# The seam between the mixers and the out pass: four raw buffers for the out weights, its first loads moved ahead of the barrier

## The reference

```python
mix = concat([y_a, y_b, y_c], -1) @ w_out          # 2048 -> 1024
x = x + rmsnorm(mix, norm_post_mix)
h = rmsnorm(x, norm_pre_ffn)
ff = (silu(h @ w_gate) * (h @ w_up)) @ w_down
return x + rmsnorm(ff, norm_post_ffn)
```

## Time and profile before

| | |
|---|---|
| median of 3 runs | 2977.15 us (2973.31 to 2978.05) |
| the profiled execution | 2977.66 us, its span 2975.5 us |
| TensorE busy | 2878.5 us, 97% of the span |
| VectorE, ScalarE, GpSimd busy | 64%, 40%, 13% |
| mean granted TensorE clock | 0.988 of full speed |

### The profile page before, as it was taken

How to read it: one execution, slowest core, us unless ns; L and a number is a source line. 1 busy time by engine, 2 the same in 40 slices (tenths; PEclk the granted TensorE clock), 3 DMA queues, 4 the chain that set the end, 5 groups by cost and what they waited for, 6 DMA issues and landing times.

```text
span 2975.5 us, 36083 instructions
## 1 busy us (share of the span) xinstructions
PE 2878.5 (97%) x13608; PEld 2314.3 (78%) x13608; DVE 1914.9 (64%) x2608; ACT 1195.8 (40%) x2005; POOL 385.7 (13%) x496
## 2 busy tenths in 40 slices
PE   8999999999999989999799999999999999999998
PEld 4888887777777667777688778888788888888887
DVE  4778787666853358888334576666776666656656
ACT  5322222354443445454333533333533333545443
POOL 0000000012530136655012100000000000000000
PEclk9999999999999999999899999999999999999999
DMA  4222343446765757876679744444542223766863
GB/s 154 68 68 90 125 132 111 136 140 198 225 202 164 254 185 244 285 264 246 251 250 347 262 181 160 155 163 160 202 166 107 107 106 135 276 219 198 296 192 107
DMA packets 294569, 545.14 MB, mean 183 GB/s; under 512 B 59228, under 2 KB 150780, under 8 KB 284924
## 3 DMA queue, kind: packets, MB, share of 16 engines
q1 hardware_dynamic: 262636, 437.69, 44.2%
q0 software_dynamic: 24704, 75.52, 6.6%
q10 hardware_dynamic: 7056, 29.63, 2.6%
HBM read 358.30 MB, written 184.44 MB: 182 GB/s over the span
## 4 chain that ended last, share of the span: by engine, by line
PE 46%; DMA 2%; DVE 2%; ACT 1%; issue 0%; SPq 0%; DVEq 0%; ACTq 0%
PE f_banks L2835 26%; PE f_banks L2843 14%; PE f_banks L2014 6%; DMA f_h_raw<-hq 1%; DMA hq<-o_tq 0%; PE f_banks L2210 0%; DMA f_bop1lo<-hq 0%; DMA f_raw<-in_w_gu 0%; DMA o_ident<-in_ident 0%; DMA f_bop6lo<-hq 0%; DVE f_bop1lo L2638 0%; DVE f_w_op L2645 0%; DVE f_snap L2671 0%; ACT f_w_op L2520 0%; ACT f_snap L2534 0%
## 5 line engine op out<-in xcount | busy, mean ns | idle before, releaser
L2843 PE MATMUL f_banks<-f_d_op 128*128 128x512 f32 x1848 | 419.0, 389 | 0.0
L2843 PEld LDWEIGHTS f_banks<-f_d_op 128*128 128x128 f32 x1848 | 347.0, 188 | 71.9
L2709 DVE TENSOR_TENSOR f_d_op<-f_d_raw,f_d_op 128x1024 fp32r<-128x1024 f32 x154 | 187.6, 1225 | 148.9 <-ACT f_d_op L2552 148.0
L1848 PE MATMUL t_banks<-t_w_hi,h_hi 128*128 128x512 f32 (+1 forms) x640 | 249.6, 390 | 8.1 <-DVE t_w_lo L1709 7.9
L656 PE MATMUL t_banks<-h_hi,c_w_hi 128*128 128x512 f32 x640 | 255.7, 400 | 0.0
L656 PE MATMUL t_banks<-h_hi,c_w_lo 128*128 128x512 f32 x640 | 249.9, 390 | 0.0
L656 PE MATMUL t_banks<-h_lo,c_w_hi 128*128 128x512 f32 x640 | 249.1, 389 | 0.0
L2552 ACT ACTIVATE f_d_op<-f_d_raw 128x1024 fp32r<-128x1024 f32 x154 | 162.8, 1061 | 198.3 <-PE f_banks L2843 163.5
L1848 PE MATMUL t_banks<-t_w_lo,h_hi 128*128 128x512 f32 (+1 forms) x640 | 238.6, 373 | 0.0
L1848 PE MATMUL t_banks<-t_w_hi,h_lo 128*128 128x512 f32 (+1 forms) x640 | 238.2, 372 | 0.0
L2534 ACT ACTIVATE f_snap<-f_banks 128x1024 f32<-128x1024 f32 x88 | 90.4, 1027 | 258.7 <-PE f_banks L2835 258.7
(11 more groups left out here) (399 smaller groups left out, 6299.5 us busy)
## 6 DMA issues: line engine op xcount, KB each, us to landing
f_raw<-in_w_gu SPq DMA_DIRECT2D x88, 512.0 KB, 6.3
sop<-f_a SPq DMA_DIRECT2D x154, 256.0 KB, 2.0
f_d_raw<-sop SPq DMA_DIRECT2D x154, 256.0 KB, 2.9
t_raw<-in_w_tok SPq DMA_DIRECT2D x72, 512.0 KB, 4.6
f_d_raw<-top SPq DMA_DIRECT2D x88, 256.0 KB, 4.3
m_bc<-rows SPq DMA_DIRECT2D x16, 1152.0 KB, 6.8
f_d_raw<-in_w_dn SPq DMA_DIRECT2D x66, 256.0 KB, 3.3
o_y_hi<-y_hi SPq DMA_DIRECT2D x16, 1024.0 KB, 5.2
```

The source lines that it names most:

```text
L1848: last = nc.tensor.matmul(banks[:, t, 0:width], h[:, b, k_first + k, tok], w[unit % 2][at][:, cols], start=begins and k == 0 and j == 0, s ...
L2709: tt(d_op[d % D_RING][:, 2:4], d_raw[:, d % S_RING], d_op[d % D_RING][:, 0:2].bitcast(F32), sub).then_inc(dlo_ok, 1)
L2843: last = nc.tensor.matmul(banks[:, bank, :], d_op[d % D_RING][:, s, tok], d_op[d % D_RING][:, w, :], start=k == 0 and j == 0, stop=k == FU ...
```

## The change

- Four raw buffers in place of two: groups 0 and 1 keep theirs, group 2 goes to `w_raw2`, which lies over the 2048 columns of `w_hi` that group 3's high part will take, group 3 to `w_raw3`, which lies over `work` and `gain_row`; group 4 takes buffer 0 again.
- SP asks for group 2 when the last mixer matmul that reads that memory is done (`c_mm`), ahead of y; for group 3 behind the first high part (`whi_ok` 1); for group 4 behind `whi_ok` 2 and `wlo_ok` 1.
- ACT makes group 3's high part ahead of `partial(15)` and first waits for group 2's low part (`wlo_ok` 3).
- y of tile 0: the low part is asked for right behind group 1, the high part at the old place.
- The three constants are loaded by SP in the first block, behind `wlo_ok` 4 and ahead of tile 1's y. x and `first` of tile 0 are loaded by POOL at the end of its program in the first block. TensorE's wait for the constants moves to its first transposes.
- Semaphores are shared or moved to match; the number of DMAs and of compute instructions stays.

```diff
@@ mixers
+    out_in0, out_in1 = sem("o_w_in0"), sem("o_w_in1")
+    out_w_in = (out_in0, 16), (out_in1, 32), (w_in, 16 * (NT // WM + 1)), (out_in0, 32), (out_in1, 48)
...
@@ mixers, sync, rest
             out_w(sp, 0)
             out_norm(sp)
             out_w(sp, 1)
+            sp.wait_ge(y_sent[0], 32)
+            out_y(sp, 0, (1,))
             sp.wait_ge(ve_ok, TT)
+            sp.wait_ge(c_mm, TT)
+            out_w(sp, 2)
             sp.wait_ge(y_ok, TT)
-            sp.wait_ge(y_sent[0], 32)
-            out_y(sp, 0)
-            for g in range(2, OGROUPS):
-                out_w(sp, g)
+            out_y(sp, 0, (0,))
+            out_w(sp, 3)
+            out_w(sp, 4)
+            out_const(sp)
             sp.wait_ge(acc_mm, TT)
             for b in range(2):
                 sp.wait_ge(y_sent[b], 32 * TT // 2)
@@ mixers, scalar, rest
                 elif c == TT:
                     out_upper(act, 2)
-            out_upper(act, 3)
+                    act.wait_ge(out_wlo_ok, 3)
+                    out_upper(act, 3)
             out_upper(act, 4)
@@ mixers, gpsimd, rest
+            pool.wait_ge(acc_mm, TT)
+            pool.wait_ge(part_sent[0], 16)
+            out_x(pool)
@@ out_memory
         y_hi, y_lo = [sb("y_hi0", [P, KM, P], F32R)], [sb("y_lo0", [P, KM, P], F32R)]
+        with ExitStack() as until:
+            until.enter_context(nc.sbuf_tensor("o_under_raw", [P, 24 * P * 2], F32))
+            w_raw2 = until.enter_context(nc.sbuf_tensor("o_w_raw2", [P, WG, NB], F32))
         w_hi = sb("w_hi", [P, OGROUPS * WG, NB], F32R)
...
-        first, work, gain_row, junk = sb("first", [P, 2, NB]), sb("work", [P, D]), sb("gain_row", [P, D]), sb("junk", [P, D], mybir.dt.bfloat16)
+        first = sb("first", [P, 2, NB])
+        with nc.sbuf_tensor("o_w_raw3", [P, WG, NB], F32) as w_raw3:
+            pass
+        work, gain_row, junk = sb("work", [P, D]), sb("gain_row", [P, D]), sb("junk", [P, D], mybir.dt.bfloat16)
...
+    w_raw = w_raw[:, 0], w_raw[:, 1], w_raw2[:], w_raw3[:], w_raw[:, 0]
@@ out_start
     def load_w(sp, g):
-        if g >= 2:
-            sp.wait_ge(wlo_ok, g - 1)
+        if g == 3:
+            sp.wait_ge(whi_ok, 1)
+        elif g == 4:
+            sp.wait_ge(whi_ok, 2)
+            sp.wait_ge(wlo_ok, 1)
         src = w_tiles[:, WG * g:WG * (g + 1), NB:D] if g < OGROUPS - 1 else w_tiles[:, 0:WG, 0:NB]
-        sp.dma_start(w_raw[:, g % 2], src).then_inc(w_in[g % 2], 16)
+        sp.dma_start(w_raw[g], src).then_inc(w_in[g][0], 16)
...
+    def load_const(sp):
+        sp.wait_ge(wlo_ok, 4)
+        for dst, src in ((gain_row[:], gain_mix.partition_broadcast(P)), (gain_col[:], gain_ffn), (ident_sb[:], ident)):
+            sp.dma_start(dst, src).then_inc(const_in, 16)
+
+    def load_x(pool):
+        pool.dma_start(xt[:, 0], x[0, 0:P, :]).then_inc(x_in, 16)
+        pool.dma_start(first[:, 0], first_dram[0:P, :]).then_inc(x_in, 16)
@@ out_pass
     def sync(sp, ahead):
-        for dst, src in ((gain_row[:], gain_mix.partition_broadcast(P)), (gain_col[:], gain_ffn), (ident_sb[:], ident)):
-            sp.dma_start(dst, src).then_inc(const_in, 16)
         for n in range(2, TT):
...
-        load(0)
         load(1)
...
         def transposes(n):
+            if n == 0:
+                pe.wait_ge(const_in, 48)
             pe.wait_ge(xn_ok, n + 1)
...
-        pe.wait_ge(const_in, 48)
         for n in range(1, TT):
```

More of the change, by code:

```diff
@@ L1952, in out_memory, with out_start @@
     return w_raw, y_hi, y_lo, w_hi, w_lo, late, tq, early, xt, x1, xn, first, work, gain_row, junk, ident_sb, stat, gain_col, norm_col
 def out_shared(sem):
-    return ((sem("o_w_in0"), sem("o_w_in1")), (sem("o_y_in0"), sem("o_y_in1")), sem("o_norm_in"), sem("o_whi_ok"), sem("o_wlo_ok"),
+    return ((sem("o_y_in0"), sem("o_y_in1")), sem("o_x_in0"), sem("o_const_in"), sem("o_whi_ok"), sem("o_wlo_ok"),
             sem("o_mm_ok"))
-def out_start(nc, shared, memory, w_out, norm_gain, yhi_dram, ylo_dram):
-    w_in, y_in, norm_in, whi_ok, wlo_ok, mm_ok = shared
-    w_raw, y_hi, y_lo, w_hi, w_lo, norm_col = memory[0], memory[1], memory[2], memory[3], memory[4], memory[-1]
+def out_start(nc, shared, memory, w_out, norm_gain, gain_mix, gain_ffn, ident, x, yhi_dram, ylo_dram, first_dram, w_in=None):
+    y_in, x_in, const_in, whi_ok, wlo_ok, mm_ok = shared
+    (w_raw, y_hi, y_lo, w_hi, w_lo, _, _, _, xt, _, _, first, _, gain_row, _, ident_sb, _, gain_col, norm_col) = memory
@@ L1974, in load_y, with load_norm @@
+    def load_norm(sp):
+        sp.dma_start(norm_col[:], norm_gain).then_inc(w_in[1][0], 16)
+    def load_y(sp, n, parts=(0, 1)):
         if n >= 2:
             sp.wait_ge(mm_ok, n - 1)
-        for dst, src in ((y_hi, yhi_dram), (y_lo, ylo_dram)):
+        for part in parts:
+            dst, src = ((y_hi, yhi_dram), (y_lo, ylo_dram))[part]
             sp.dma_start(dst[n % 2][:].bitcast(F32), src[n]).then_inc(y_in[n % 2], 16)
-    def load_norm(sp):
-        sp.dma_start(norm_col[:], norm_gain).then_inc(norm_in, 16)
+    def load_const(sp):
+        sp.wait_ge(wlo_ok, 4)
+        for dst, src in ((gain_row[:], gain_mix.partition_broadcast(P)), (gain_col[:], gain_ffn), (ident_sb[:], ident)):
+            sp.dma_start(dst, src).then_inc(const_in, 16)
@@ L1988, in upper @@
                 scale = norm_col[:, k - UT:k - UT + 1] if k < UT + GK else 1.0
[L1989 removed]
+                ins = nc.scalar.activation(w_hi[:, k, :], w_raw[g][:, k % WG], ACT.Copy, scale=scale)
         else:
[L1991 removed]
+            ins = nc.scalar.activation(w_hi[:, WG * g:WG * (g + 1), :], w_raw[g], ACT.Copy)
         ins.then_inc(whi_ok, 1)
@@ L2016, in products @@
         last.then_inc(mm_ok, 1)
-    return load_w, load_y, load_norm, upper, lower, products
+    return load_w, load_y, load_norm, load_const, load_x, upper, lower, products
 def out_pass(nc, sem, shared, memory, banks, tr_banks, x, w_out, norm_gain, gain_mix, gain_ffn, ident, yhi_dram, ylo_dram, first_dram,
@@ L2026, in out_pass @@
     (w_raw, y_hi, y_lo, w_hi, w_lo, late, tq, early, xt, x1, xn, first, work, gain_row, junk, ident_sb, stat, gain_col, norm_col) = memory
[L2027 to L2030, removed]
+    x_in0, const_in, _, wlo_ok, mm_ok = shared[1:]
+    _, load_y, _, _, _, _, _, products = out_start(nc, shared, memory, w_out, norm_gain, gain_mix, gain_ffn, ident, x, yhi_dram, ylo_dram,
+                                                   first_dram)
+    x_in = x_in0, sem("o_x_in1")
     x1_sent, h_sent = (sem("o_x1_sent0"), sem("o_x1_sent1")), [sem("o_h_sent%d" % r) for r in range(2 * QT)]
```

21 lines of the change are left out of this document (10 added, 11 removed).

## The result

| | before | after |
|---|---|---|
| median (4 runs each) | 2975.83 us (2973.31 to 2978.05) | 2958.97 us (2957.89 to 2961.20) |
| span of the profiled execution | 2975.5 us | 2956.7 us |
| mean granted TensorE clock | 0.988 | 0.991 |

The ratio is 0.9943, with a 95% interval of 0.9931 to 0.9954: 16.9 us between the medians, 14 to 20.5 by the interval; 18.8 us between the spans. Two later comparisons gave 0.9938 [0.9925, 0.9950] and 0.9942 [0.9930, 0.9955]. The forecast was 2958.4 us. Over all executions of the two kernels, in four comparisons, the means are 2976.9 us (33 of before) and 2959.2 us (14 of after): 17.7 us, within about 1.2.

What follows compares the result with a forecast made beforehand. TensorE, busy 97% of the span, bounds the kernel; only idle and low-clock time can be won. Seam 37.44 us to 13.81 + 1.83 + 0.40 + 2.62 = 18.66, so 2977.15 - 18.8 = 2958.4 us; range 2953.5 to 2965.5.

Steps and rivals of the forecast that it cites:

- products: Tile 0's products in the out pass: weight groups 2 to 4 arrive in time and TensorE runs through in 13.81 us.
- barrier: Between the two blocks: TensorE sets the barrier and is through it 1.83 us after tile 0's products.
- 12 starts: First twelve matmuls of tile 1's products: they start within 2.62 us, at full clock.
- The clock: Restart after the seam's gap of 1.8 to 2.2 us: full clock, as after the 2.04 us gap; before, 2.2 and 2.1 us lost.
- The second y: Tile 1's y, issued at 1438.3: flies 10.7 us, lands at 1449.0, a wait of 0.4 us; bounds none to 1.8 us.
- Rival A: Seam: tile 1's y lands late or the restart is at 1.2 GHz; 3.5 us less gain, 2961.9 us; chance 0.19.
- First y ... nothing: Tile 0's y, low part early and high part as now: both there long before 1432.99, worth nothing.
- a group's slack: Weight groups against TensorE's need: group 2 6.4 us to spare, group 3 4.7 us, group 4 hidden or 1.1 us late.
- the store of `first`: Ahead of group 4's low part, which waits for it: flight taken as 4 us, 7.8 at worst.
- x of tile 0: Loaded by POOL before the barrier: `xn` there at about 1460, before tile 1's products end at 1462.7; hidden.
- Rivals B to E: B: weight group stops TensorE (0.05); C: gain given back later (0.06); D: no change (0.03); E: slower (0.03).
- Rival B: Tile 0's products: a weight group still stops TensorE, group 4 1.1 us late, 2959.5 to about 2964 us; chance 0.05.

Runs made afterwards that it cites:

- kernels with one half each: Before kernel with only the weights' buffers, their order and y's order changed, 2968.31 us (0.9971); or only constants, x and `first` loaded early, 2967.13 us (0.9967).
- filled wait: The kernel with the weights alone plus 28 matmuls of no use ahead of TensorE's wait for the constants: 2966.64 us, ratio to before 0.9965.
- three of the experiments: Changed kernel with `partial(15)` ahead of group 3's high part, 2960.44 us; with tile 0's y whole at the old place, 2961.22; with both, 2961.64.
- two other orders of the same loads: Weights' buffers and orders changed but constants and x late, 2968.31 us; changed kernel with tile 1's y asked for ahead of the constants, 2962.76 us.
- first y whole: Changed kernel with the low part of tile 0's y back with the high part, ahead of groups 3 and 4: 2961.22 us, ratio to before 0.9952.
- second y first: Changed kernel with tile 1's y asked for ahead of the three constants, without waiting for group 3's low part: 2962.76 us, ratio to before 0.9953.
- weights alone: Changed kernel with constants, x and `first` of tile 0 and TensorE's wait for the constants as before: 2968.31 us, ratio to before 0.9971.
- three buffers: Changed kernel with three raw buffers, group 3 in buffer 1 again and asked for behind group 1's low part: 2960.28 us, ratio to before 0.9945.

## Why the prediction was right

**The mechanism and the sum.** Forecast and measured, from first to 72nd matmul: products 13.81 and 13.80 us (1433.42 to 1447.22), barrier 1.83 and 1.76, wait for y 0.40 and none, 12 starts 2.62 and 2.61; in all 18.66 and 18.18. 2958.4 against 2958.97 us. That the times agree to 0.6 us is in part luck: the forecast was taken from 2977.15 us, and the median of before with a fourth run is 2975.83, so the gain is 16.9 us by these medians and 17.7 over all executions, against 18.8. The kernels with one half each show that both halves are paid about as forecast, 9.8 and 9.0 us forecast, 9.2 and 10.4 by the medians and 8.4 and 12.0 in the traces, where the first met a wait of 1.2 us and the second had shorter waits for weights.

**The clock.** Two waits were entered twice, as idle time and as 1.2 GHz, 4.3 us in all. The filled wait shows that this is right: the same 8.8 us between the products without idling cost 2.2 us less. That the restart would be at full clock was a choice between two rows, 2.04 us and 2.57; it came out in all nine profiles where the barrier alone stood behind tile 0's products (1.76 or 1.77 us), but no run shows why, and the last section has gaps that went the other way.

**The second y.** 10.7 us of flight taken, 9.4 measured; the 0.40 us was the one term with the wrong value of any size. It is a close race all the same: it was lost in three of the experiments (gaps of 2.73, 2.74 and 3.88 us), with 2.6 to 4.6 us each, idle time and clock. The estimate from the Trainium skill's rate (DMA: Bandwidth & Descriptors, Anatomy of one DMA) had y there at 1444.5; it landed at 1448.0. The row, with 1449.0, was nearer than the page, though that nothing would wait came out as by the page. (By that estimate the gain would be 0.4 us larger, and the sum smaller, not larger as the prediction says.) Rival A was real, and missed by 1 us.

**What was wrong in it, and hidden by the result.** "First y ... nothing" does not hold: its low part out of the busy stretch saves group 3 five us of flight, without which the seam is 3.1 us longer. The order of `partial(15)`, which I did not price alone, is worth 2.6. The step that failed is the same: a group's slack was worked out against TensorE alone (4.7 us for group 3), while SP's next loads hang on the same event. Along this chain the slack was 1 us. For group 4 I did see that the store of `first` decides; I took 4 us for its flight and 7.8 at worst, measured were 4.8 in the change and 9.5 at worst.

**x of tile 0** was costed at nothing because it is hidden in its new place. That is right, and says nothing about its worth: left at the old place it costs about 6 us in the trace.

**Rivals B to E.** None of them appeared in the changed kernel. Rival B's wait for group 4 came in two other orders of the same loads. In the profiles nothing was given back later (1505.12 and 1505.15 us behind the 72nd matmul); the executions leave room for about 1 us.

## What to carry to other kernels

When a group's lateness is worked out, list every wait on its event, the DMA queue's own among them: the shortest slack here was not TensorE's. When loads are moved forward, ask which small store they overtake: 2 MB issued 0.2 to 0.6 us ahead of a 256 KB store doubled its flight, 4.8 to 9.5 us. And when a large wait is taken away, move whatever it used to hide along with it, or the gain stops at the next one.

## What was not expected of the hardware

In the seam, gaps of 1.76 us were followed by a full clock in every profile that has one, and that of 2.04 us in the earlier trace rows too; those of 2.31, 2.73 and 2.74 us were followed by 1.2 GHz. But length alone does not tell. Earlier in the program, where TensorE waits for `t_w_lo`, a gap of 3.73 us in the kernel with the first y whole kept its clock, and one of 1.79 us in the kernel with the second y first did not keep it long:

```profile
1021.82 0.50 PE L1860 MATMUL t_banks<-t_w_hi,h_hi 128*128 128x512 f32 x1 [3.73 <-DVE t_w_lo L1721]
1021.80:1024.30 2.50, 1.64 (x6) 1.05 (x6) 1.72 (x2) 1.44 (x2) 0.00 (x0) 1.00 0.55 116
```

```profile
985.75 0.50 PE L1861 MATMUL t_banks<-t_w_hi,h_hi 128*128 128x512 f32 x1 [1.79 <-DVE t_w_lo L1722]
987.00:990.30 3.30, 3.30 (x6) 1.59 (x5) 1.35 (x2) 0.63 (x1) 0.00 (x0) 0.50 1.00 387
```

In each pair the second row is the stretch behind the gap (its last three figures are granted clock, DMA share and GB/s). In the kernel with the weights alone the wait of 3.0 us in the channel mixer kept its clock. TensorE's row, and then windows (length, busy us by engine, granted clock, DMA share, GB/s):

```profile
1686.27 0.50 PE L2862 MATMUL f_banks<-f_bop1hi,f_w_op 128*128 128x512 f32 x1 [3.04 <-DVE f_w_op L2672]
```

The stretch behind it, and one behind the next such wait:

```profile
1686.30:1690.00 3.70, 3.70 (x16) 3.08 (x17) 3.31 (x3) 2.60 (x6) 0.75 (x1) 1.00 1.02 416
1697.00:1700.00 3.00, 3.00 (x10) 2.38 (x11) 2.93 (x3) 3.00 (x5) 0.00 (x0) 0.71 1.02 418
```

The next one, 4.0 us long and ended at 1696.93, did not: 0.71 in the second row is a mean over both levels. In the changed kernel the gap at the first of these places was 2.88 us and did cost the clock:

```profile
1675.70:1678.00 2.30, 2.30 (x6) 1.82 (x7) 1.88 (x2) 2.30 (x6) 0.75 (x1) 0.52 1.03 424
```

So a gap of about 3 us can go either way at the same place, and what a gap will cost in clock is not to be had from its length in these traces.

The 1 MB load of a weight group took from 5.2 us (group 3 in the kernel with three buffers) to 17.2 us (group 3 behind the whole y of tile 0, with 1.5 MB of stores issued after it) to land, so one flight time for a kind of transfer is not to be had from the trace of before; asking later can be free, as three buffers showed.
